# Order of copies and low parts in two causal attentions, and the mixture's low parts within its products

## The reference, cut to what matters

```python
gates = jax.nn.sigmoid(jnp.concatenate([ga, gc], axis=-1) + b_gate[i])
gate_attn, gate_conv = jnp.split(gates, 2, axis=-1)
mixed = (gate_attn * y_attn + gate_conv * y_conv) @ w_o[i]
...
s = einsum('bqhd,bkhd->bhqk', q_i, k) * scale      # + log_f_cum[t] - log_f_cum[s] in the forget attention
p = softmax(where(key_pos <= q_pos, s, -inf))
out = einsum('bhqk,bkhd->bqhd', p, v)
```

## Time and profile before

| | us |
|---|---|
| median of 3 runs | 3236.27 |
| lowest, highest | 3231.32, 3238.64 |
| profiled execution | 3228.07 |
| its span | 3226.3 |
| busy TensorE (PE) | 2966.4 (92%) |
| busy VectorE (DVE) | 1699.0 |
| busy ScalarE (ACT) | 1201.3 |
| busy GpSimd (POOL) | 1050.7 |

### The profile page before, as it was taken

The page is one execution under the profiler, slowest core; times in us unless marked ns, Lnnn a source line. Parts: engine busy times, 40 slices in busy tenths (PEclk is TensorE's granted clock), DMA queues, the critical chain, the costliest instruction groups (busy, mean ns, idle before and its releaser), DMA issues.

```text
span 3226.3 us, 36561 instructions
## 1 busy us (share of the span) xinstructions
PE 2966.4 (92%) x14426; PEld 2438.0 (76%) x14426; DVE 1699.0 (53%) x1733; ACT 1201.3 (37%) x1959; POOL 1050.7 (33%) x418
## 2 busy tenths in 40 slices
PE   5988999998999999999989999999898899889996
PEld 3777778887778888888767887777776677777785
DVE  4777742112243434443578546777735766665433
ACT  3666710001231101011144234777734455556521
POOL 3211135444424444444433233111122311211252
PEclk9999999999999999999999999999999999999998
DMA  2010021112111111111112212100121100010221
GB/s 102 21 34 33 33 105 46 53 46 98 46 33 46 46 52 46 52 46 48 57 53 87 81 56 75 72 20 19 35 79 72 46 27 27 27 33 20 85 105 65
DMA packets 42570, 171.65 MB, mean 53 GB/s; under 512 B 4464, under 2 KB 5488, under 8 KB 41392
## 3 DMA queue, kind: packets, MB, share of 16 engines
q1 hardware_dynamic: 32976, 119.90, 11.6%
q10 hardware_dynamic: 9440, 49.55, 3.9%
HBM read 143.74 MB, written 25.69 MB: 53 GB/s over the span
## 4 chain that ended last, share of the span: by engine, by line
PE 75%; issue 10%; DVE 8%; ACT 5%; POOL 1%; DMA 0%; ACTq 0%; SPq 0%; DVEq 0%; POOLq 0%
PE ps L535 45%; PE ps L1160 5%; PE ps L716 4%; PE ps L923 3%; PE aux L1051 3%; PE ps L986 2%; PE ps L1035 2%; PE ob L1077 1%; PE ob L1080 1%; PE ob L1078 1%; PE ob L748 1%; PE aux L736 1%; PE ps L736 1%; POOL wh L478 1%; PE ob L766 1%
## 5 line engine op out<-in xcount | busy, mean ns | idle before, releaser
L478 POOL TENSOR_TENSOR wh<-raw,con 128x1024 fp32r<-128x1024 f32 x203 | 495.9, 2443 | 2105.4 <-PE ps L535 935.8
L480 POOL TENSOR_TENSOR wl<-raw,wh 128x1024 fp32r<-128x1024 f32 x203 | 547.0, 2695 | 15.9
L535 PE MATMUL ps<-hh,wh 128*128 128x512 f32 x1344 | 421.8, 395 | 27.5 <-POOL wl L480 15.2
L535 PE MATMUL ps<-hl,wh 128*128 128x512 f32 x1344 | 418.0, 392 | 0.0
L535 PE MATMUL ps<-hh,wl 128*128 128x512 f32 x1344 | 417.8, 392 | 0.0
L535 PEld LDWEIGHTS ps<-hh,wh 128*128 128x128 f32 x1344 | 254.5, 191 | 84.3 <-POOL wl L480 16.9
L535 PEld LDWEIGHTS ps<-hl,wh 128*128 128x128 f32 x1344 | 255.2, 190 | 53.8
L535 PEld LDWEIGHTS ps<-hh,wl 128*128 128x128 f32 x1344 | 254.9, 190 | 53.6
L1888 DVE TENSOR_TENSOR px_l<-px,px_h 128x512 fp32r<-128x512 f32 (+3 forms) x288 | 205.3, 715 | 121.5 <-ACT px_h L1702 119.4
L1405 ACT ACTIVATE ff<-fr 128x1024 f32<-128x1024 f32 x32 | 33.9, 1061 | 552.5 <-DVE fr L2121 552.5
L2132 DVE TENSOR_TENSOR y_t<-y_t,ps 128x1024 f32<-128x1024 f32 x120 | 146.5, 1221 | 172.9 <-PE ps L535 172.9
(11 more groups left out here) (439 smaller groups left out, 6308.0 us busy)
## 6 DMA issues: line engine op xcount, KB each, us to landing
raw<-wall SPq DMA_DIRECT2D x211, 512.0 KB, 3.5
spill_x<-x_t ACTq DMA_DIRECT2D x2, 4096.0 KB, 12.1
xold_t<-spill_x ACTq DMA_DIRECT2D x2, 4096.0 KB, 13.2
x_t<-xt SPq DMA_DIRECT2D x8, 512.0 KB, 10.4
spill_o<-op ACTq DMA_DIRECT2D x4, 1024.0 KB, 4.0
o_all<-spill_o ACTq DMA_DIRECT2D x2, 2048.0 KB, 11.8
x_t<-xt ACTq DMA_DIRECT2D x1, 4096.0 KB, 14.0
spill_out<-ot ACTq DMA_DIRECT2D x8, 512.0 KB, 2.6
```

The costliest lines, as they stand in the source:

```text
L478: pool.tensor_tensor(wh[:, s, :, :], raw[:, s, :, :], ones.unsqueeze(1).broadcast_to([P, KT, P]), ALU.mult).then_inc(w_high, 1)
L480: pool.tensor_tensor(wl[:, s, :, :], raw[:, s, :, :], wh[:, s, :, :].bitcast(F32), ALU.subtract).then_inc(w_split, 1)
L535: m = pe.matmul(ps[:, w, a:b], lw[:, sl, k, :], r[:, i, a:b], start=(i == 0 and j == 0), stop=(i == len(ks) - 1 and j == 2))
```

## The change

The mixture: ScalarE loads the table and copies tiles 0 to 6 as soon as the last gate is out and seven sums are made, and only tile 7 waits for the last sum; the load of `x_t` is issued after it. VectorE takes the low part of tile 0 before the last m's first multiply, those of tiles 1 to 4 before its second, and 5 to 7 after the sum. The attentions: ScalarE's `tile` now has, in this order, both exponentials, the diagonals, the copy of the row, the log of the sums and its inverse. MLA: the low part of the values moves from step 7 to 8, that of the keys from 6 to 10. Forget attention: keys are projected one step earlier (10 to 15) and evacuated in step 15; copies are split in two, first those that the maxima read, with the others one to three steps later under semaphores of their own (`fqc_ready`, `fkc_ready`), which the scores and the next evacuation wait for; the low part of the keys of a pair's first head moves from step 18 to 21.

```diff
-    B_ACT = {1: "shift", 2: "abs", 3: "exp", 4: "ln", 9: "q", 10: "k", 15: "vt", 16: "v"}
+    B_ACT = {1: "shift", 2: "abs", 3: "exp", 4: "ln", 9: "q", 10: "k", 11: "q copy", 12: "k copy", 15: "vt", 16: "v"}
...
-    FOX_PARTS = {a + i: (piece, *ks) for a, piece in ((0, "v"), (9, "q"), (16, "k"))
+    FOX_PARTS = {a + i: (piece, *ks) for a, piece in ((0, "v"), (9, "q"), (15, "k"))
...
-    FOX_OUT = {5: "v", 7: "vt", 14: "q", 21: "k"}
+    FOX_OUT = {5: "v", 7: "vt", 14: "q", 20: "k"}
...
-    FOX_ACT = {2: ("q", 1), 3: ("k", 1), 5: ("v", 1), 13: ("q", 2), 15: ("v", 2), 17: ("k", 2)}
-    FOX_DVE = {2: ("bias", 1), 3: ("q", 1), 4: ("k", 1), 6: ("v", 1), 14: ("bias", 2), 15: ("q", 2), 16: ("v", 2), 18: ("k", 2)}
+    FOX_ACT = {2: ("q", 1), 3: ("k", 1), 4: ("q copy", 1), 5: ("v", 1), 6: ("k copy", 1),
+               12: ("q", 2), 14: ("q copy", 2), 15: ("v", 2), 16: ("k", 2), 18: ("k copy", 2)}
+    FOX_DVE = {2: ("bias", 1), 3: ("q", 1), 4: ("k", 1), 6: ("v", 1), 14: ("bias", 2), 15: ("q", 2), 16: ("v", 2), 21: ("k", 2)}
...
             pe.wait_ge(fqx_ready, h + 1)
             pe.wait_ge(fkx_ready, h + 1)
+            pe.wait_ge(fqc_ready, h + 1)
+            pe.wait_ge(fkc_ready, h + 1)
...
+        act.preload_act_table_set("natural_log_exp_and_others")
+        act.wait_ge(tile_ready, base + KT - 1)
+        for k in range(KT - 1):
+            copy(hh[:, k, :], mix_t[:, k, :]).then_inc(high_ready, 1)
         act.wait_ge(work_done, t.now("work"))
         act.wait_ge(tile_ready, base + KT)
+        copy(hh[:, KT - 1, :], mix_t[:, KT - 1, :]).then_inc(high_ready, 1)
         act.dma_start(x_t[:, :, :], xt.rearrange("(k p) s -> p k s", p=P)).then_inc(xold_in, 16)
-        act.preload_act_table_set("natural_log_exp_and_others")
-        for k in range(KT):
-            copy(hh[:, k, :], mix_t[:, k, :]).then_inc(high_ready, 1)
...
                     exponential(step)
-                if last_of_chunk(done, heads):
-                    log_sum(done)
-                if 0 <= step < heads * N_HT:
                     high_part(step)
                 for block_of in maxima_of(step, heads):
                     diagonal(*block_of)
-                if last_of_chunk(done, heads):
-                    inverse_sum(done)
-
-            def row(step):
                 rh, rc = row_of(step, heads)
                 if rh is not None:
                     maxima_row(rh, rc)
+                if last_of_chunk(done, heads):
+                    log_sum(done)
+                    inverse_sum(done)
...
             if what == "q":
-                copy(fqx[h % 2][rows, :], fqr[rows, :])
                 copy(fqb[h % 2][rows, :], fqr[rows, :]).then_inc(fq_ready, 1)
+            elif what == "k":
+                copy(fkb[h % 2][rows, :], fkr[rows, :]).then_inc(fk_ready, 1)
+            elif what == "q copy":
+                copy(fqx[h % 2][rows, :], fqr[rows, :]).then_inc(fqc_ready, 1)
             else:
-                copy(fkx[h % 2][other, :], fkr[rows, :])
-                copy(fkb[h % 2][rows, :], fkr[rows, :]).then_inc(fk_ready, 1)
+                copy(fkx[h % 2][other, :], fkr[rows, :]).then_inc(fkc_ready, 1)
...
+        def mix_low(k):
+            dve.wait_ge(high_ready, t.next(high_ready))
+            low(hl[:, k, :], mix_t[:, k, :], hh[:, k, :]).then_inc(tile_split, 1)
+
         for m in range(KT):
             wa, wc = t.take("work"), t.take("work")
+            last = m == KT - 1
+            if last:
+                mix_low(0)
             w, slot = work()
             evacuated(wa)
             dve.tensor_tensor(ga[:, :], ps[:, slot, :], ga[:, :], ALU.mult).then_inc(work_free[slot], 1)
+            if last:
+                for k in range(1, 5):
+                    mix_low(k)
             w2, slot = work()
...
-        for k in range(KT):
-            dve.wait_ge(high_ready, t.next(high_ready))
-            low(hl[:, k, :], mix_t[:, k, :], hh[:, k, :]).then_inc(tile_split, 1)
+        for k in range(5, KT):
+            mix_low(k)
...
-        parts = {2: latent_rope, 4: latent_q_low, 6: latent_k_low, 7: latent_v_low}
+        parts = {2: latent_rope, 4: latent_q_low, 8: latent_v_low, 10: latent_k_low}
```

More of the change, by code:

```diff
@@ L289, in program @@
         map(sem, ("fq_ready", "fk_ready", "fbias_ready", "fqx_ready", "fkx_ready", "fvh_ready", "fvl_ready"))
+    fqc_ready, fkc_ready = map(sem, ("fqc_ready", "fkc_ready"))
     gate_out, gate_in = [sem(f"gate_out{i}") for i in range(2)], sem("gate_in")
@@ L1745, in send @@
                     t.take(ot_out, 16)
-            return tile, row, send
+            return tile, send
         latent_q_nope(0)
@@ L1759, in _ @@
         act.preload_act_table_set("natural_log_exp_and_others")
-        tile, maxima_row_out, _ = softmax(MLA_HEADS, MLA_MAX, dg, inv, lambda h: qa[h % 2][0][96:P, :])
+        tile, _ = softmax(MLA_HEADS, MLA_MAX, dg, inv, lambda h: qa[h % 2][0][96:P, :])
         def y_high(m):
@@ L1772, in _ @@
                 parts[i](h + 1)
-            maxima_row_out(step)
             if step == FETCH_STEP:
@@ L1804, in fox_row @@
             return fqb[h % 2][a:a + 32, :]
-        fox_tile, fox_maxima_row, fox_send = softmax(2 * FOX_PAIRS, FOX_MAX, fdg, finv, fox_row)
+        fox_tile, fox_send = softmax(2 * FOX_PAIRS, FOX_MAX, fdg, finv, fox_row)
         fox_base = t.now("tiles") - 2 * FOX_PAIRS * N_HT
@@ L1810, in fox_high @@
             pair, rows, other = h // 2, (LO, HI)[h % 2], (HI, LO)[h % 2]
-            act.wait_ge(fpiece_free, fox_number("vt" if what == "v" else what, pair) + 1)
+            act.wait_ge(fpiece_free, fox_number("vt" if what == "v" else what[0], pair) + 1)
             if what == "v":
@@ L1850, in _ @@
             fox_tile(step)
-            fox_maxima_row(step)
             piece, pair = fox_step(step, FOX_OUT)
@@ L2548, in fox_out @@
                 dve.wait_ge(fqx_ready, 2 * pair)
+                if pair > 0:
+                    dve.wait_ge(fqc_ready, 2 * pair)
                 out_ = dve.scalar_tensor_tensor(out=fqr[:, :], in0=ps[:, FOX_SLOT, :], scalar=SCALE_64, in1=by_row[:, :],
@@ L2553, in fox_out @@
                     dve.wait_ge(fkx_ready, 2 * pair)
+                    dve.wait_ge(fkc_ready, 2 * pair)
                 dst = fkr if piece == "k" else fvt
```

## The result

The changed kernel takes 3199.74 us (median of four runs, 3197.73 to 3204.26), the kernel before 3234.99 beside it: a ratio of 0.9888, 95% interval 0.9869 to 0.9907, so 1.1% faster. The forecast was 3197 with 3178 to 3222. The profiled execution took 3197.73 us, its span is 3195.9, the granted clock 0.98. TensorE is busy 2957.6 us for 2966.4: what went is idle time and time at the lower clock.

A forecast was written before the change was run, and what follows sets the result against it. TensorE bounds the kernel, busy 2966.4 of 3226.3 us. Mixture 9.5 plus forget attention 32 less MLA 2 gives 39.5 us gained: 3188.6 from the profiled execution, 3197 from the median 3236.27, range 3178 to 3222.

The forecast's parts named there:

- The residual of 1 us: Mixture's end: TensorE still waits about 1 us at tile 5 for its low part, leaving 9.5 us gained.
- the low part of the keys goes past the split, 4.4 us a transition and the clock: Forget attention: third maximum comes 4.4 us earlier in four transitions, 17.6 us, and the clock gives back 9 us.
- The `fkb` term: Forget attention: with `fkb` copied first, the first maximum comes only 0.6 us earlier, not 1.62.
- third maximum, head with the split, `k_low` in step 10: MLA: third maximum 1.2 us earlier in ten heads, -12; split head and last head's row, -4; next head's scores, +1.
- `v_low` in front of the fourth reduction: MLA: the values' low part delays the fourth reduction, so the fifth maximum waits about 1 us: +10 us.
- `qf` behind the row: MLA: `qf` queues behind ScalarE's wait for the row's product, so `ckv` starts 0.7 us later in ten heads: +7 us.
- The new wait of `ckv_h` for `qf`: MLA, sign of the forecast: a new wait of about 1.1 us in ten heads.
- The first (MLA gains too): Rival: MLA's stops of 27 us mostly go, 15 to 20 us more gained, 3179; chance 0.17.
- The second (a new wait takes half of Fox's gain): Rival: in the forget attention ScalarE's 3 us wait for the row reaches TensorE and the clock falls, 3217; chance 0.22.
- The third: Rival: slower, ScalarE's idle time before the row's copy is passed on in full in both attentions, 3250; chance 0.03.
- The fourth: Rival: the mixture doesn't overlap, TensorE stalls again in tile 5 for 4 us, 3202; chance 0.08.
- what would have shown the forecast wrong: MLA's idle time falling by over 10 us, or a `px_h` wait of a microsecond or more in each pair.

The follow-up runs named there:

- y3: The changed kernel with the forget attention's low part of the keys back in step 18: 3202.37 us, ratio to before 0.9894.
- u1: The kernel before with only the forget attention's low part of the keys moved from step 18 to 21: 3211.68 us, ratio 0.9934.
- u2: The kernel before with the forget attention's key projection a step earlier and its copies split, keys' low part still in step 18: 3229.20 us, ratio 0.9983.
- x2: The kernel before with only ScalarE's new order inside a step, in both attentions: 3216.40 us, ratio 0.9940.
- y4: The changed kernel with the forget attention's key projection, its evacuation and `fkb` a step later, as before: 3196.10 us, ratio to before 0.9881.
- z2: The changed kernel with ScalarE's old order in MLA and the values' low part back in step 7: 3188.24 us, ratio to before 0.9846.
- x3: The kernel before with only MLA's low parts moved (values' from step 7 to 8, keys' from 6 to 10): 3231.08 us, ratio 0.9985.
- y2: The changed kernel with MLA's low part of the values back in step 7: 3196.31 us, ratio to before 0.9869.
- z1: The changed kernel, but in MLA ScalarE makes `qf` before row, log and inverse, and the values' low part is in step 7: 3182.64 us, ratio to before 0.9833.
- x4: The kernel before with the forget attention's earlier key projection, split copies and keys' low part in step 21, ScalarE's order old: 3205.02 us, ratio 0.9904.

## Why the prediction was right, and where it was not

**Mixture: right in size, and in its steps but for one length.** 9.3 us for 9.5. The residual of 1 us is the measured 1.00, at the tile that was named. Its make-up is only in part the forecast one: `mix_t` took 2.10 us, since it met a split, as the text allowed (0.9 more than alone), but the larger part is the low part of tile 5 itself, 3.42 us where the sum had about 1.25. So the size of the residual is right, with some luck in it. The low part of tile 0 took 2.71 us. The Trainium skill, SBUF — State Buffer, "Who interferes with whom", would have made it 8.5, by the prediction's own estimate; the subtractions did meet the splits, but in front of tile 5 VectorE had the time. Its sentence that the later instruction waits is borne out on either side by rows of this study: `fkx` took 3.37 where the split was first, and the split 3.48 where `fkx` started with it (y3). Here too the splits that met the low parts and the sum took 2.95 and 3.26 us for 2.40.

**Forget attention: right in size (32.1 for 32), and its terms are not the separate causes they were added up as.** The step "the low part of the keys goes past the split, 4.4 us a transition and the clock" is a true mechanism: alone it gives 22.4 us (u1), where 17.6 + 9 of the sum hung on it. But it was taken for the only one, and this is the flaw of the sum, which no term shows. "VectorE sits in the low part of the keys" named one of the two stretched subtractions; the other, `px_l`, stood in the same timeline, and ScalarE's order, which I had costed as a loss of some of the gain, gives 20.9 alone by bringing it ahead of the split. The 3.73 us wait needs both, and each of the two moves ends most of it (1.20 left by the order, 0.4 to 0.5 by the low part's move). That is why undoing the low part's move in the changed kernel costs only 1.7 us (y3). The `fkb` term was too small: the prediction had the first maximum 0.6 us earlier in each transition, and the wait of 1.62 went whole. Split copies and earlier projection are worth 9.3 us on the kernel before (u2) and 9.5 on top of the order (x2's 396.6 less y3's 387.1); of the two it is the copies as far as y4 shows, since the earlier projection is worth nothing in the changed kernel. Taken in this order the runs make 20.9 (ScalarE's order) + 9.5 (copies and projection) + 1.7 (step 21) = 32.1; begun with step 21, that move would show 22.4. The forecast put 26.6 of its 32 on that move and nothing on the order in the first four pairs, so that the total agrees to 0.1 us is in part luck. (The prediction also likened all 21 waits for the reductions to the one of 3.73 us: four in Fox and one of 3.6 in MLA are so long.)

**MLA attention: right in sign, mis-sized, by terms that erred in both directions.** Runs price each step of the sum against its neighbour (of the 4 us in the first row about half a microsecond is the last head's row, which goes with the order and not with `k_low`):

| step of the prediction | forecast, us | measured | from |
|---|---|---|---|
| third maximum, head with the split, `k_low` in step 10 | -12 - 4 + 1 = -15 | -7.3 | z2 less before |
| `v_low` in front of the fourth reduction | +10 | +5.4, +5.7 | x3 less z2; changed less y2 |
| `qf` behind the row | +7 | +8.2 | y2 less z2 |
| sum | +2 | +6.7 | changed less before |

The step that failed is the third maximum: "without it, 1.2 earlier in ten heads". The wait did shrink by 1.1 us (1.55 to 0.43, 1.33 to 0.20, in z2), but a head came out only 0.5 us shorter: a part went to the next stops, the 512 wide maximum (0.18, in every other head) and `px_h` (0.17).

```profile
2124.35 0.44 PE L1037 MATMUL ps<-ka_h,qa_h 96*128 96x384 f32 x1 [0.43 <-DVE small L2428]
```

The rest of the difference is not traced. The waits of `v_low` were overpriced for the same reason, 0.8 us a head and not 1.0, and half of that net. The new wait of `ckv_h` for `qf` was forecast at 1.1 us in ten heads and stands at 1.29 in ten. The order costs 8.2 us with `k_low` in step 10, and 0.6 with it in step 6 (x2): as a price it holds only next to the other move, which is how the sum used it. All these differences carry the 3 us within which the same instructions vary.

**Rivals.** The first (MLA gains too) fell for the reason given: the row's product is behind the exponentials. It describes z1, though: with `qf` taken out from behind that wait and `v_low` in step 7, MLA gains 9.9 us on the kernel before. The second (a new wait takes half of Fox's gain) fell; the wait for `px_h` exists, 4.6 us in all and mostly in the last pair, and the clock stays up. The third needed both attentions to pass ScalarE's idle time on in full; MLA passed on 8.2 us of its 25, Fox nothing that shows. The fourth fell: tile 5 waited 1.00 us and not 4, although the sum did meet a split.

Of what would have shown the forecast wrong, neither came: TensorE's idle time in MLA rose from 29.9 to 33.5 us and did not fall by 10, and no wait for `px_h` of a microsecond stands in each pair.

## What to carry to other kernels

When a wait is traced to one long instruction, list everything between the wait's start and its release on the releasing engine: here two stretched subtractions made one wait of 3.7 us, and two different edits, each moving another thing, cured most of it: 20.9 and 22.4 us alone, 32.1 together and with all the rest. One of them needed only that a subtraction start 0.3 us ahead of a split and not 0.4 behind it, and in y3 0.06 us decided between 1.21 and 3.43 us, so compare the starts of the two instructions, not only their lengths. Prices of edits are thus conditional; undoing one edit in the changed kernel (1.7 us) and doing it alone (22.4 us) answer different questions, and only both show that two edits do one job. In an in-order queue put an instruction that the next product needs ahead of one that must itself wait for a product, and those that only release late buffers (log, inverse) behind both: that gave 11 us in MLA (345.1 in y2, 334.2 in z1) and another 5 in Fox. For the log of MLA the last part is not shown: z2, with the log in front, is only 2.7 us behind z1.

## What the runs showed of the hardware that was not expected

The sums over columns ahead of MLA (32 products of one column) ran at two speeds with the same instructions. TensorE's timeline, first before:

```profile
1992.81 3.71 PE L600 MATMUL ob<-con,sq 128*128 128x1 f32 x32
1996.38 0.71 PE L986 MATMUL ps<-cq_h,wh 128*128 128x512 f32 x2
```

and then after:

```profile
1984.39 5.05 PE L602 MATMUL ob<-con,sq 128*128 128x1 f32 x32
1989.31 1.20 PE L988 MATMUL ps<-cq_h,wh 128*128 128x512 f32 x2
```

Busy time by stretch (columns as in the earlier trace rows), before:

```profile
1993.00:1996.00 3.00, 3.00 (x29) 3.00 (x28) 1.16 (x1) 0.00 (x0) 2.89 (x2) 1.00 0.00 0
```

and after:

```profile
1981.00:1984.00 3.00, 3.00 (x15) 2.48 (x14) 0.91 (x1) 0.00 (x0) 0.00 (x0) 1.00 0.00 0
1987.00:1990.00 3.00, 3.00 (x14) 2.90 (x15) 0.20 (x1) 0.27 (x1) 2.35 (x1) 0.50 0.00 0
```

The granted clock goes from 1.00 to 0.50, which is from 2.4 to 1.2 GHz, within the sums, although TensorE has been busy in full for the 12 us before them; in the kernel before, with the same 12 busy microseconds, it stays at 1.00. (In both kernels the clock is 0.50 when these 12 us begin, and it has been back at 1.00 for 8 us when the sums do.) The products behind run at half speed too (1.20 for 0.71). It costs 3.3 us: GpSimd's splits are 8.4 us early in front of the place and 5.1 behind it. Of the fourteen profiles, five have 3.71 us (before, x2, x3, x4, u2) and nine 4.89 to 5.05 (all that have the mixture's part, and u1, which has not). They also part by when the sums start: at 1992.8 us of the span or later in the five, at 1989.9 or earlier in the nine. Why the clock falls in some is open, and no run was made for it. The Trainium skill, TensorE: Matmul & The Clock Gate, "What's actually happening", says that the monitor behind the clock runs on its own time and does not start with the kernel, so that the moment of a change differs from run to run; that would allow a fall in some profiles and not in others, and no run here shows it. A second place lies at 1573 us of the changed kernel's span (1584 before): behind an idle time of 2.51 us that both kernels have, products of 512 columns meet a clock of 0.52 over 3 us in the changed kernel and of 1.00 before, which costs 1.6 us. Twelve of the fourteen profiles lose this time, all but before and u1; x2, x3, x4 and u2, which have the old instructions here, are among the twelve. A change that speeds up one stage can so lose some of it in an untouched one, which a comparison stage by stage shows and one of totals does not.
